# Gate rounds of a two-block kernel: ScalarE writes the weighted one-hot rows of every eighth unit, and its PSUM copies no longer wait for their own end

## What is computed

```python
idx = jnp.take_along_axis(cand_idx, pos, axis=-1)
gates = jax.nn.softmax(top_s, axis=-1).astype(h.dtype)
...
u = expert_down[ib]
act = jax.nn.gelu(jnp.einsum("td,thkd->thk", hb, u), approximate=False)
v = expert_up[ib]
return jnp.einsum("thk,thkd->td", gb * act, v)
```

## Time and profile before

| | |
|---|---|
| median of 3 runs | 2797.38 us (2790.15 to 2800.26) |
| the profiled execution: its own time | 2797.25 us |
| its span, first to last instruction | 2795.6 us |
| PE busy, of the span | 2662.6 us (95%) |
| DVE busy | 1805.1 us (65%) |
| ACT busy | 943.1 us (34%) |
| gate rounds, first to last unit on PE | about 748.6 to 919.6 us |

### The profile page before, as it was taken

How to read it: one execution, slowest core, us unless ns; L and a number is a source line. 1 busy time by engine, 2 the same in 40 slices (tenths; PEclk the granted TensorE clock), 3 DMA queues, 4 the chain that set the end, 5 groups by cost and what they waited for, 6 DMA issues and landing times.

```text
span 2795.6 us, 35889 instructions
## 1 busy us (share of the span) xinstructions
PE 2662.6 (95%) x12743; PEld 2118.7 (76%) x12743; DVE 1805.1 (65%) x3276; ACT 943.1 (34%) x1219; POOL 829.2 (30%) x530
## 2 busy tenths in 40 slices
PE   5999989999999999999999999999999999899997
PEld 3455445599877789999999887699877877688875
DVE  6842766699999688888888898550118533560532
ACT  2323223333477333233322222453233233332321
POOL 2100001155300134444444322244222243244442
PEclk7999999999999999999999999999999999999998
DMA  8511334333355799999999888223624432122321
GB/s 343 181 57 61 110 122 168 128 124 120 101 199 195 271 333 336 331 336 333 337 334 337 300 303 309 100 83 114 107 80 154 150 113 90 60 98 91 98 90 60
DMA packets 194874, 507.16 MB, mean 181 GB/s; under 512 B 31312, under 2 KB 83552, under 8 KB 192720
## 3 DMA queue, kind: packets, MB, share of 16 engines
q1 hardware_dynamic: 146608, 326.99, 35.7%
q0 software_dynamic: 48160, 178.87, 17.7%
HBM read 456.58 MB, written 49.22 MB: 181 GB/s over the span
## 4 chain that ended last, share of the span: by engine, by line
PE 63%; issue 16%; DVE 12%; POOL 5%; DMA 1%; ACT 1%; DVEq 1%; SPq 0%; POOLq 0%; ACTq 0%
PE psum L1681 19%; PE psum L1983 14%; PE psum L1668 13%; PE psum L547 6%; PE psum L562 6%; POOL l_r L890 5%; DVE arena L2053 3%; DVE arena L2050 2%; DVE look_oh L2050 2%; DVE arena L2057 1%; PE psum L1407 1%; PE psum L1990 1%; DVEq L2053 1%; DVE arena L2402 1%; DVE arena L2403 1%
## 5 line engine op out<-in xcount | busy, mean ns | idle before, releaser
L915 ACT ACTIVATE arena<-psum 128x512 f32<-128x512 f32 (+8 forms) x474 | 320.6, 687 | 1106.8 <-PE psum L1668 345.6
L2050 DVE TENSOR_TENSOR arena<-arena 128x384 f32<-128x384 f32 (+8 forms) x399 | 307.8, 777 | 493.2 <-ACT arena L915 265.7
L1681 PE MATMUL psum<-e_r,e_r 128*128 128x512 f32 x2304 | 541.1, 393 | 7.0 <-DVE e_r L2050 7.0
L890 POOL TENSOR_TENSOR l_r<-arena,l_r 128x1024 fp32r<-128x1024 f32 x144 | 351.1, 2439 | 655.3 <-ACT l_r L500 655.3
L1668 PE MATMUL psum<-e_r,e_r 128*128 128x384 f32 x2048 | 532.4, 340 | 4.5 <-ACT arena L915 2.4
L1681 PEld LDWEIGHTS psum<-e_r,e_r 128*128 128x128 f32 x2304 | 434.5, 189 | 96.2 <-issue 4.6
L915 ACT ACTIVATE e_r<-arena 128x1024 fp32r<-128x1024 f32 x256 | 270.3, 1057 | 367.9 <-PE psum L1681 346.6
L1668 PEld LDWEIGHTS psum<-e_r,e_r 128*128 128x128 f32 x2048 | 364.4, 188 | 15.5 <-POOL l_r L860 6.3
L1668 PE MATMUL psum<-e_r,l_r 128*128 128x384 f32 x1024 | 343.8, 336 | 0.0
L874 POOL DMA_INDIRECT arena<-in_down_rows,arena x128 | 160.3, 1253 | 431.4 <-DMA scratch_early<-arena 192.9
L874 POOL DMA_INDIRECT arena<-in_up,arena x128 | 162.1, 1266 | 247.8 <-DVE arena L2539 122.1
(11 more groups left out here) (230 smaller groups left out, 3321.3 us busy)
## 6 DMA issues: line engine op xcount, KB each, us to landing
arena<-in_down SPq DMA_DIRECT2D x128, 512.0 KB, 4.9
arena<-in_up SPq DMA_DIRECT2D x128, 512.0 KB, 6.7
scratch_gates<-arena SPq DMA_DIRECT2D x12, 2048.0 KB, 7.3
arena<-scratch_gates SPq DMA_DIRECT2D x30, 768.0 KB, 10.0
arena<-in_w_in SPq DMA_DIRECT2D x44, 512.0 KB, 3.6
arena<-in_w_ada POOLq DMA_DIRECT2D x40, 512.0 KB, 6.0
arena<-in_w_query SPq DMA_DIRECT2D x16, 512.0 KB, 3.5
arena<-in_w_glu SPq DMA_DIRECT2D x16, 512.0 KB, 3.6
```

The costliest lines, as they stand in the source:

```text
L890: nc.gpsimd.tensor_tensor(rr(lo, 1024, "l"), reg(RING + q % NSLOT * SLOT, 1024), rr(hi, 1024, "l").bitcast(F32), ALU.subtract).then_inc(S[ ...
L915: do(sc.activation(out, in_, f, **kw), sem)
L1681: last = mm(bank(2 * tt_ + hf), rr(w__ + tt_ * P, P), rr(x__ + hf * 512, 512), start=(first and n == 0), stop=(final and n == 2))
L2050: do(v.tensor_tensor(out, a, b, op), sem)
```

## The change

ACT takes over matrix B of the last unit of each round (unit 7 of 0 to 7). That matrix lies in an area of its own, `small[:, 96:608]`, one 128x128 part for each of its four tokens. For one token ACT computes the distance of each column from i2 (Abs), and then Relu(gate - gate * distance), which is the gate where the distance is 0 and 0 elsewhere. The scale, minus the gate, is copied once ahead of the rounds to `minus_g`. ACT's loop over a round has four turns with two units each; turn i writes the part of token i, Abs ahead of the copy of its first unit and Relu between its two copies. DVE writes only A for unit 7, and its second half of each round is written out without a loop. PE waits at unit 7 also for the four Relus (`b_hotx`). ACT's copies no longer wait for their own end. `mag8` moves to another place in `small`.

```diff
+    def settle(self, sem):
+        if self.i is None:
+            self.eng.wait_ge(self.sems[sem], self.sems.base(sem) + self.base[sem])
+        else:
+            self.eng.wait_ge(self.sems[sem], self.i * self.per[sem] + (self.sems.base(sem) + self.base.get(sem, 0) + self.k[sem]))
...
+            wait("slots_T", 3)
+            act_(minus_g.rearrange("p (c t) -> p c t", c=NGC),
+                 reg(GT, TD).rearrange("p (c x t) -> p c x t", c=NGC, x=8)[:, :, 7, :], ACT.Copy, scale=-1.0)
...
-                with tn.loop(8 // GB, g_evac=GB) as i:
+                with tn.loop(8 // GB, g_evac=GB, act_own=1, b_hotx=1) as i:
+                    hot = small[:, bass.ds(i * P + OBX, P)]
+                    act_(hot, con("iota"), ACT.Abs, "~act_own", scale=-1.0, bias=A[:, bass.ds(i + (I2T + 32 * c + 28), 1)])
                     for u_ in range(GB):
                         wait("g_mm", i * GB + (GB + c * 8 + u_ + 1))
                         act_(stg[:, bass.ds(i * (4 * GB) + 4 * u_, 4), :],
-                             bank(u_).rearrange("p (t j) -> p t j", t=4), ACT.Copy, "g_evac")
+                             bank(u_).rearrange("p (t j) -> p t j", t=4), ACT.Copy, "~g_evac")
+                        if u_ == 0:
+                            tn.settle("act_own")
+                            act_(hot, hot, ACT.Relu, "~b_hotx", scale=small[:, bass.ds(i + (608 + 4 * c), 1)],
+                                 bias=A[:, bass.ds(i + (GT + 32 * c + 28), 1)])
                 if c == NGC - 1:
+                    wait("g_evac", GB + TD // 4)
...
                     pe.wait_ge(S["g_evac"], S.base("g_evac") + i * (8 * NSLOT) + (x + 1))
+                    if x % 8 == 7:
+                        pe.wait_ge(S["b_hotx"], S.base("b_hotx") + i * (4 * NSLOT) + 4 * (r + 1))
                     for t in range(4):
                         last = mm(bank(u_)[:, t * P:(t + 1) * P], reg(OA + u_ * 512 + t * P, P),
-                                  reg(OB + u_ * 512 + t * P, P), start=True, stop=True)
+                                  small[:, OBX + t * P:OBX + (t + 1) * P] if x % 8 == 7 else reg(OB + u_ * 512 + t * P, P),
+                                  start=True, stop=True)
...
+                if c % 2 == 0:
+                    with tn.loop(4 // GB, b_hot=GB) as i:
...
+                else:
+                    for n in range(4 * c, 4 * c + 4):
+                        u_ = n % GB
+                        wait("g_mm", n + 1)
                         tt(three(OA + u_ * 512, 4, P), bc(con("iota").unsqueeze(1), [P, 4, P]),
+                           bc(reg(I1T + 4 * n, 4).unsqueeze(2), [P, 4, P]), ALU.is_equal,
+                           "~b_hot" if n % 8 == 7 else FREE)
+                        if n % 8 < 7:
+                            for t in range(4):
+                                ts(reg(OB + u_ * 512 + t * P, P), con("iota"), reg(I2T + 4 * n + t, 1),
+                                   reg(GT + 4 * n + t, 1), ALU.is_equal, ALU.mult, "~b_hot" if t == 3 else FREE)
```

More of the change, by code:

```diff
@@ L139 @@
                    ("gq", 4), ("ff_split", 32)],
-    "act_6": [("u_hi", 128), ("l_hi", 144)],
+    "act_6": [("b_hotx", 48), ("u_hi", 128), ("l_hi", 144)],
     "pool_1": [("l_lo", 144)],
@@ L346, in build @@
         OA, OB = UHI, UHI + GB * 512
+        OBX = 96
+        minus_g = small[:, 608:656]
         GATH = PV
@@ L422, in build @@
         dtx, dt_t, dt_2, dt_s = (small[:, 464 + 64 * n:528 + 64 * n] for n in range(4))
-        mag8 = small[:, 256:320]
+        mag8 = small[:, 32:96]
         g_sq, g_mid = gsc[:, 8:16], mod[:, 0:8]
@@ L2490, in _ @@
             for c in range(2 * NGC):
[L2491 to L2494, removed]
-                        tt(three(OA + u_ * 512, 4, P), bc(con("iota").unsqueeze(1), [P, 4, P]),
[L2496 to L2500, removed]
+                if c % 2 == 0:
+                    with tn.loop(4 // GB, b_hot=GB) as i:
+                        for u_ in range(GB):
+                            n = 4 * c + u_
+                            wait("g_mm", i * GB + (n + 1))
+                            tt(three(OA + u_ * 512, 4, P), bc(con("iota").unsqueeze(1), [P, 4, P]),
+                               bc(A[:, bass.ds(i * (4 * GB) + (I1T + 4 * n), 4)].unsqueeze(2), [P, 4, P]), ALU.is_equal, FREE)
+                            for t in range(4):
+                                ts(reg(OB + u_ * 512 + t * P, P), con("iota"),
+                                   A[:, bass.ds(i * (4 * GB) + (I2T + 4 * n + t), 1)],
+                                   A[:, bass.ds(i * (4 * GB) + (GT + 4 * n + t), 1)], ALU.is_equal, ALU.mult,
+                                   "~b_hot" if t == 3 else FREE)
+                else:
+                    for n in range(4 * c, 4 * c + 4):
+                        u_ = n % GB
+                        wait("g_mm", n + 1)
+                        tt(three(OA + u_ * 512, 4, P), bc(con("iota").unsqueeze(1), [P, 4, P]),
+                           bc(reg(I1T + 4 * n, 4).unsqueeze(2), [P, 4, P]), ALU.is_equal,
+                           "~b_hot" if n % 8 == 7 else FREE)
+                        if n % 8 < 7:
+                            for t in range(4):
+                                ts(reg(OB + u_ * 512 + t * P, P), con("iota"), reg(I2T + 4 * n + t, 1),
+                                   reg(GT + 4 * n + t, 1), ALU.is_equal, ALU.mult, "~b_hot" if t == 3 else FREE)
```

## The result

The changed kernel takes 2802.80 us (median of 20 runs), the kernel before 2792.18 us (20 runs; the three shown earlier had 2797.38). The ratio is 1.0036, 95% interval 1.0027 to 1.0046: slower by 10 us, between 7.5 and 12.8. Its profiled execution took 2804.45 us, with a span of 2802.8.

A forecast was written before the change was run, and what follows sets the result against it. DVE was taken to bound the gate rounds; the late Relu at unit 7 costs eleven rounds 1.00 us and the last 1.18, 12.2 us, giving 2809.6 us. Own range 2803 to 2817, whole range 2799 to 2819.

The forecast's parts named there:

- What bounds: Gate rounds: they go at DVE's pace, 1.63 us a unit, with the double buffer binding almost as tightly.
- The cap: DVE at the next round's first unit: waiting for unit 6's matmuls limits the 1.02 us saving to 0.18 us a round.
- ACT's own waits at zero: ACT's copies in the rounds: dropping the waits for their own end gains zero, at most 0.18 us.
- The new wait at unit 7: PE at unit 7: the fourth Relu stands behind unit 6's copy, so unit 7 follows unit 6 by 2.81 us, not 1.63.
- DVE's unit behind it: DVE's second unit of the next round: it waits for unit 7's matmuls and starts 1.00 us late.
- The sum: All twelve rounds: eleven pass on 1.00 us, the last 1.18, together 12.2 us slower, 2809.6 us.
- the lower bound I had named: The twelve rounds: a Relu of 0.30 us, without the cost of operands, makes the loss 10.0 us.
- the 14 us that I had set for calling it slower: Whole kernel: about 0.5% can be told from no change, so slower means above 2811.4 us, given 0.37.
- ACT's load at zero: ACT in the rounds: 2.7 us more work a round costs zero; PE's 0.4 us wait, if uncovered, would be 4.8 us.
- The rule of the Trainium skill: Relu work moved from DVE to ACT: by the rule alone no gain; four tokens need 1.02 us on DVE, 2.7 on ACT.
- The clock: PE in the rounds: stays at 1.00; the rival, a fall after the new gap, costs 16 us more, 2826, chance 0.05.

The follow-up runs named there:

- e1: The changed kernel with ACT's Abs and Relu taken out of the rounds, unit 7's B rows written once ahead; ratio 0.9981 to the kernel before, 2787.20 us.
- e2: The changed kernel with each Relu ahead of the first copy of its turn, right behind its Abs; ratio 0.9999 to the kernel before, 2792.65 us.
- e6: The changed kernel with ACT's loop written out, Abs and Relus behind the copies of units 2 to 5; ratio 0.9999 to the kernel before, 2792.78 us.
- e3: The kernel before with only the waits of ACT's copies for their own end taken away; ratio 0.9996, 2792.82 us.
- e4: The changed kernel with the own waits of ACT's copies put back; ratio 1.0111 to the kernel before, 2825.28 us.
- e7: The changed kernel with Abs and Relus behind the copies of units 2 to 5 and low_d behind unit 7; ratio 0.9956 to the kernel before, 2780.65 us.
- e9: As e7, with the own waits of ACT's copies put back; ratio 0.9977 to the kernel before, 2784.10 us.

## Why the prediction was right

By its steps:

- **What bounds.** Right. DVE had no idle time before, and with less work and the Relu in time (e1, e2, e6) the round was shorter by only 0.14 us. The cap was forecast at 0.18.
- **ACT's own waits at zero.** Right for the edit by itself (e3). Not said was that in the changed order the edit is needed; e4 shows it.
- **The new wait at unit 7.** Right in its place, links and releaser. Of the terms, 1.16 + 0.13 and 0.05 came as forecast. The copy holds ACT for 0.86 us instead of 0.99: it takes 1.06 us, not 1.09, and the next instruction overlaps it by 0.20, not 0.10. The Relu takes 0.46, not 0.48. The chain is 2.66 us and not 2.81.
- **DVE's unit behind it.** Forecast 1.00 us a round late, measured 0.88 as the mean length. Its idle times were forecast at 0.84 and about 1.2, measured 0.85 and 0.93.
- **The sum.** 12.2 us forecast, 10.7 to 11.0 by the traces and 10 by the ratio. That 10.0 was also the lower bound I had named is chance: it stood on a Relu of 0.30 us, and what was shorter was mostly the copy. The 2809.6 us missed 2802.8 by more than that, because it stood on a median of three that lies 5.2 us above the median of twenty. For the same reason 2802.8 lies just below the forecast's own range (2803 to 2817) and only within the wider one (2799 to 2819). In the chain itself no two errors cancelled: the copy and the Relu both came out shorter. The difference of 10 us is clear of zero, and under the 14 us that I had set for calling it slower.
- **ACT's load at zero.** Right. PE waits up to 0.30 us for the copy of the next round's first unit before it starts the third (forecast 0.4), and it goes no further. No table loads came in: there are 42 in either trace. e2 has 12.10 us of ACT in a round of 14.00 and loses nothing.
- **The rule of the Trainium skill** ("ScalarE: Activation LUTs", "Rules for kernel authors": relu, max, add and mul go to VectorE, not ScalarE). The trace agrees that DVE is the faster of the two for this work, 0.26 us a token against 0.38 + 0.46 for ACT's two instructions. For the change its "no gain" came true, but not for its reason. As a rule on where the work should lie it would have misled: e7 does the same slow work on ACT and is 12 us faster than before, since DVE and not ACT bounds the rounds.
- **The clock.** It did not fall in the change, as forecast: it was 1.00 from 760 to 932 us. The argument for this compared unlike gaps, though, 1.4 us between weight loads with 1.08 us between matmuls. Like with like, the longest weight-load gap of a round was 1.40 us before (at 800.24) and is 1.30 us at unit 7 now, and PE's own gap 1.08 and 0.98: nothing longer than before came in, though such a gap now stands twice a round and not once. That longer gaps do bring it down is shown by e4.

## What to carry to other kernels

To take work off the engine that bounds a stage is worth only what its next instruction can start earlier. Look at what that instruction waits for, here the matmuls of two units before, and have other work ready that doesn't wait for it. Work that moves to another engine should be put ahead of that engine's last wait, not behind it, when someone needs it soon: the same eight instructions a round cost 10 us with the last one behind unit 6's copy, nothing in the middle of the round, and gained 12 us there once `low_d` filled the gap. Even there they must not make their engine late (e9).

## What the runs showed of the hardware

- The overlap of one ACTIVATE with the next is larger behind this transposing copy out of PSUM, 0.20 us (818.56 + 1.06 against 819.42), than the 0.10 us behind gelu and `hi_d`. Why was not tested.
- A wait for an instruction's own end costs ACT about 0.27 us from start to start where nothing is computed behind it (1.13 in e9 against 0.86 in e7). In a loop with address instructions behind it, it costs about 0.42 within a turn (1.28 in e4 against 0.86 in the change) and 0.60 at the turn's end (822.17 to 823.65, 1.48 us, against 0.88, 816.93 to 817.81).
- PE idle for 0.98 us before unit 7 in every round left its clock at 1.00 in the change behind the first round; 2.52 us in e4 were followed by units of 1.84 and 1.59 us.
